# GpSimd takes over the subtraction for 36 weight pieces beside a 31-tap convolution

## The reference, cut to what matters

```
h   = rms_norm(x, norm_mix_pre)                  # 256 x 2048
u   = h @ w_in_2                                 # 2048 -> 4352 = 3*768 + 2*768 + 512
u_a, u_b, u_c = split(u)
val, gate = split(u_b); glu = val * sigmoid(gate)
y_b = silu(layer_norm(causal_conv31(glu) + bias))  # 31 taps per channel, 768 channels
y_a = b_gate * causal_conv3(c_gate * v)            # from u_a
y_c = pooled means of u_c, times pool_w
y   = concat(y_a, y_b, y_c) @ w_out_2
```

## Time and profile before

| | us |
|---|---|
| median of 3 runs | 2858.72 |
| profiled execution, its own time | 2861.59 |
| span of its instructions | 2859.5 |
| TensorE busy (matmul) | 2675.6 |
| VectorE busy | 1665.1 |
| ScalarE busy | 1158.2 |
| GpSimd busy | 10.6 |

### The profile page before, as it was taken

The page is one execution under the profiler, slowest core; times in us unless marked ns, Lnnn a source line. Parts: engine busy times, 40 slices in busy tenths (PEclk is TensorE's granted clock), DMA queues, the critical chain, the costliest instruction groups (busy, mean ns, idle before and its releaser), DMA issues.

```text
span 2859.5 us, 45648 instructions
## 1 busy us (share of the span) xinstructions
PE 2675.6 (94%) x20456; PEld 2552.4 (89%) x20456; DVE 1665.1 (58%) x1955; ACT 1158.2 (41%) x1266; POOL 10.6 (0%) x23
## 2 busy tenths in 40 slices
PE   6899999999989999999999799849699999999996
PEld 3488898899989999999999699839599999999996
DVE  4266666387767545455454457954566546654664
ACT  3222555343335434344343343323444434443442
POOL 0000000000000000000000000000000000000000
PEclk9899999999999999999999899969799999999998
DMA  9766565487765655555555244415155555555451
GB/s 375 306 234 229 199 220 192 162 297 273 293 235 215 225 180 184 186 179 190 177 185 184 103 148 154 153 51 188 55 181 181 188 181 188 177 186 183 177 192 45
DMA packets 76211, 546.91 MB, mean 191 GB/s; under 512 B 8720, under 2 KB 8848, under 8 KB 11120
## 3 DMA queue, kind: packets, MB, share of 16 engines
q1 hardware_dynamic: 73424, 533.53, 51.5%
q0 software_dynamic: 2304, 9.96, 0.9%
q10 hardware_dynamic: 288, 0.50, 0.1%
HBM read 538.72 MB, written 5.24 MB: 190 GB/s over the span
## 4 chain that ended last, share of the span: by engine, by line
PE 86%; DVE 8%; DMA 2%; ACT 2%; issue 1%; SPq 0%; POOL 0%; ACTq 0%; DVEq 0%
PE acc L264 24%; PE acc L266 24%; PE acc L268 24%; DVE cacc L1178 2%; PE mp L450 2%; DVE wlo L232 2%; DMA raw<-in_w_mod 2%; PE acc L284 2%; PE acc L285 1%; PE acc L286 1%; PE mp L286 1%; PE mp L284 1%; PE mp L285 1%; PE mp L333 1%; DVE macc L377 1%
## 5 line engine op out<-in xcount | busy, mean ns | idle before, releaser
L232 DVE TENSOR_TENSOR wlo<-raw,whi 128x1024 fp32r<-128x1024 f32 x813 | 984.2, 1223 | 875.3 <-ACT whi L222 873.1
L222 ACT ACTIVATE whi<-raw 128x1024 fp32r<-128x1024 f32 x813 | 853.6, 1058 | 1347.7 <-PE acc L268 1153.4
L264 PE MATMUL acc<-hh,whi 128*128 128x256 f32 x3616 | 1034.5, 286 | 37.0 <-issue 23.7
L266 PE MATMUL acc<-hl,whi 128*128 128x256 f32 x3616 | 1025.6, 284 | 0.0
L268 PE MATMUL acc<-hh,wlo 128*128 128x256 f32 x3616 | 1025.4, 284 | 0.0
L264 PEld LDWEIGHTS acc<-hh,whi 128*128 128x128 f32 x3616 | 695.9, 192 | 48.9 <-issue 39.2
L266 PEld LDWEIGHTS acc<-hl,whi 128*128 128x128 f32 x3616 | 696.2, 193 | 1.2 <-issue 1.0
L268 PEld LDWEIGHTS acc<-hh,wlo 128*128 128x128 f32 x3616 | 695.8, 192 | 0.0
L264 PE MATMUL acc<-mh,whi 128*128 128x256 f32 x2240 | 631.4, 282 | 16.5 <-DVE ml L1262 15.1
L268 PE MATMUL acc<-mh,wlo 128*128 128x256 f32 x2240 | 633.6, 283 | 0.0
L266 PE MATMUL acc<-ml,whi 128*128 128x256 f32 x2240 | 633.6, 283 | 0.0
(11 more groups left out here) (242 smaller groups left out, 1706.6 us busy)
## 6 DMA issues: line engine op xcount, KB each, us to landing
raw<-in_w_in SPq DMA_DIRECT2D x98, 1024.0 KB, 4.8
raw<-in_w_mod SPq DMA_DIRECT2D x96, 1024.0 KB, 5.0
raw<-in_w_up SPq DMA_DIRECT2D x88, 1024.0 KB, 4.8
raw<-in_w_mlp_in SPq DMA_DIRECT2D x64, 1024.0 KB, 4.8
raw<-in_w_mlp_out SPq DMA_DIRECT2D x64, 1024.0 KB, 4.7
raw<-in_w_down SPq DMA_DIRECT2D x44, 1024.0 KB, 4.7
raw<-in_w_out SPq DMA_DIRECT2D x32, 1024.0 KB, 4.8
raw<-in_w_fourier_out SPq DMA_DIRECT2D x8, 1024.0 KB, 4.9
```

What stands on the lines that cost most here:

```text
L222: nc.scalar.activation(whi[:, r, :], raw_slot(k)[:, 2 * GC * j:2 * GC * (j + 1)], ACT.Copy)\
L232: nc.vector.tensor_tensor(wlo[:, r, :], raw_slot(k)[:, 2 * GC * j:2 * GC * (j + 1)], whi[:, r, :].bitcast(f32), ALU.subtract).then_inc(S[" ...
L264: nc.tensor.matmul(dst, whi[:, r, cols], hi[:, kt, :], start=begin, stop=False, skip_group_check=True)
L266: nc.tensor.matmul(dst, whi[:, r, cols], lo[:, kt, :], start=False, stop=False, skip_group_check=True)
```

## The change

GpSimd gets a loop at the end of its program that makes the low halves of 36 pieces in a row, from piece `P_TAPS` on. Its instruction is the same subtraction of 128x1024 values. It waits for `hi_n` as VectorE did, and also for `lo_n` to have reached p, so that the count goes on from VectorE's last piece and then from its own. `P_TAPS` is four above the first piece of u_a, since the low halves run four pieces ahead: the 36 are the last 32 pieces of `w_in_2` and the first 4 of `w_out_2`.

VectorE no longer makes any piece in that stretch. In each of the four groups it goes through 48 steps of the convolution without a piece between them, then waits for the group and copies it. Before the last copy it waits until `lo_n` shows all 36 pieces.

```diff
+P_TAPS = len(PIECE) - 2 * (16 + 22 * 4 + 44) - 36 + 4
...
+        def pool_piece(pool, p):
+            k, j = PIECE[p]
+            pool.wait_ge(S["hi_n"], p + 1)
+            pool.wait_ge(S["lo_n"], p)
+            nc.gpsimd.tensor_tensor(wlo[:, p % 4, :], raw_slot(k)[:, 2 * GC * j:2 * GC * (j + 1)],
+                                    whi[:, p % 4, :].bitcast(f32), ALU.subtract).then_inc(S["lo_n"], 1)
...
+            for p in range(P_TAPS, P_TAPS + 36):
+                pool_piece(pool, p)
...
             for g in range(0, 2):
                 for b in range(2):
-                    C(behind=taps(g, 48 * b))
+                    assert st.p == P_TAPS + 8 * (2 * g + b)
+                    add = taps(g, 48 * b)
+                    for _ in range(8):
+                        add()
+                    st.p += 8
+                    st.e += 8
                     group_done(dve, st)
                     nc.vector.tensor_copy(uT[:, ds(8 * g + 4 * b, 4), :], tiles(acc[b][:, :]))\
                         .then_inc(acc_free[b], 1)
-            C(4)
+            st.p += 4
+            st.e += 4
+            dve.wait_ge(S["lo_n"], st.p)
             group_done(dve, st)
```

## The result

The changed kernel takes 2893.91 us (median of 4 runs, 2891.48 to 2896.98) against 2858.95 us for the kernel before (4 runs). The ratio is 1.0121, with a 95% interval of 1.0103 to 1.0138. The forecast was 2891.8 us. The profiled execution took 2895.22 us and has a span of 2893.4 us.

The account below looks back on a forecast made before the run. VectorE was taken to bound the 118.4 us convolution stretch. There 79.2 us of GpSimd pieces plus 72.3 us of convolution make 151.5 us, 33.1 us longer, so 2858.72 us becomes 2891.8 us; range 2844 to 2912 us.

Parts of the forecast that it names:

- What is removed: VectorE's queue in the convolution stretch: 36 pieces by 1.135 us, 40.9 us, leaving 77.5 us of convolution and copies.
- Taking turns: Convolution stretch: GpSimd pieces and VectorE's two-SBUF-input steps exclude each other by whole instructions; 33.1 us longer, chance 0.58.
- The size: Convolution stretch: 79.2 us of pieces plus 72.3 us of convolution, 151.5 us against 118.4 us now.
- the price of a piece: One low-half subtraction on GpSimd: 2.2 us, halfway between two streams and three, with ends 0.95 and 2.66 us.
- two inputs in turn: A GpSimd subtraction reading its inputs one after the other, with the output beside them, would cost 1.8 us.
- the overlap at hand-overs: Between a GpSimd piece and a convolution step: could hide 0.13 us at most 36 times, or cost as much; left out.
- The stalls: TensorE in the convolution stretch: about 47 us idle in three or four blocks over 10 us, waiting for a copy, clock dropping.
- VectorE first: Rival: GpSimd gets nothing while a group's 48 steps run; stretch 26.3 us longer, 2885.0 us, chance 0.08.
- free passage: Rival: in the convolution stretch the engines don't meet and TensorE sets the pace; gain 12.6 us, 2846.1 us, chance 0.20.
- Less the 11.0 us of waits this becomes 1853.9 us: End of TensorE's last piece in the stretch, about 1864.9 us, moved earlier by its waits for low halves.

Follow-up runs that it names:

- the sums in PSUM: Changed kernel with the convolution's two running sums in PSUM instead of SBUF, one extra copy per tile: 2843.16 us, ratio 0.9935 to the kernel before.
- the fill: Kernel before, VectorE still making all pieces, plus 36 unused GpSimd fills of 1024 values beside the convolution: 2863.66 us, ratio 1.0007.
- The copy: Kernel before, VectorE still making all pieces, plus 36 unused GpSimd copies of 1024 values, one SBUF input each: 2885.89 us, ratio 1.0088.
- the run with 16 pieces: Changed kernel with only 16 of the 36 pieces on GpSimd, in the first two groups, VectorE making the other 20: 2877.06 us, ratio 1.0054.
- no steps: Changed kernel without the convolution's 174 multiply-adds, which are replaced by signals: 2838.89 us, ratio 0.9925 to the kernel before.
- the run with the later wait: Changed kernel with running sums in PSUM and VectorE's wait for all 36 low halves moved behind the mixer: 2838.99 us, ratio 0.9918.

## Why the prediction was right, step by step

**What is removed.** 40.9 us of VectorE's queue were forecast, and 77.5 us to remain. The run with the sums in PSUM shows about the same: VectorE was busy for 80.63 us in the stretch, with 2.5 us of added copies in it. One slip is in how I divided the 77.5 us. The last copy, 0.61 us, starts at 1869.80 us, where the stretch ends, so the convolution had 72.9 us and not 72.3, and the sum should have been 152.1 us.

**Taking turns** is shown, by three independent runs: take the second SBUF input away from VectorE and the loss is gone (0.47 us a step); take the inputs away from GpSimd (the fill) and it is gone (0.458 us); keep both, without any dependence, and it is there (2.10 us for a step that waited). The rule of the Trainium skill that I named (SBUF — State Buffer, § Who interferes with whom) agrees with each of the three, also in that a GpSimd instruction that only writes leaves the steps alone.

**The size** came out right (74.0 us forecast to be added, 154.2 - 77.5 = 76.7 measured) with two errors that cancel. The first is the price of a piece. I took 2.2 us; it is 2.40 us, and 2.55 us from start to start. I had reasoned that no row shows GpSimd hiding one stream behind another. The copy shows it: one stream in and one out took 1.04 us, hardly more than the fill's 0.954. By that a subtraction would be the 1.8 us of two inputs in turn. It took 1.89 us with one tensor and 2.40 us with three, so my 2.2 us was near for no good reason. My estimate of 2.25 us from the figure of the Trainium skill (GPSIMD Engine Reference, § 3.1 Elementwise) was also too low for the three tensors of this change. The second is how a piece meets VectorE. I hid the copies beside pieces, 5.2 us, and left out the overlap at hand-overs as at most 4.7 us. In fact all copies fell where GpSimd was idle, and in each turn one step went along at no cost of its own: 36 x 2.55 + 77.5 - 36 x 0.39 = 155.3 us. Counted from VectorE's side, 36 instructions were held, one for each piece: 33 multiply-adds at 2.61 us (2.15 us more than a free one), two of L1182 at 2.38 and one of L1175 at 2.50 us. This is 2.13 us for each piece (76.7/36), which my 2.2 us met by luck.

**The stalls** were forecast as about 47 us of idle time in three or four blocks of over 10 us, with the clock falling. Measured: TensorE idle for 154.22 - 103.61 = 50.6 us, of which 37.0 us lay in three waits for a copy, the longest 15.8 us, and 12.9 us in a fourth before the small matmuls; TensorE's granted clock was 0.50, the lower level of 1.2 GHz, from 1800 to 1810 us. They cost nothing beside the sum, as the run with 16 pieces shows.

**VectorE first** did occur once. The piece that started at 1847.22 us lasted 7.95 us, through 15 undisturbed steps from 1847.25 on, while each other piece got in after at most one step. Why this one didn't is open. It made the loss no smaller: like the others it held one instruction of VectorE in the end, the addition L1175 at 1852.95 us, for 2.50 us.

**What was wrong: the rival "free passage"**, in its size. I gave it 2846.1 us, a gain of 12.6 us; where passage was free the gain was 18.2 and 22.4 us (the sums in PSUM, and no steps). The step that failed is "Less the 11.0 us of waits this becomes 1853.9 us". That row doesn't hold all that TensorE lost: for the same 808 matmuls its modelled busy time was 104.82 us before and 98.10 us in the run with the sums in PSUM, so some of the loss was counted as busy. The count gives it rightly. The stretch has 796 large matmuls (808 less the 12 small ones), at 0.12 us each, as the chain shows them where TensorE isn't held up:

```profile
1840.09 0.12 PE acc L273
1840.21 0.12 PE acc L275
```

That is 95.5 us. With the sums in PSUM TensorE took 95.4 us from the end of the gated product (1748.54) to the small matmuls (1843.89), where the kernel before had taken 113.4 us (1751.45 to 1864.87), 18.0 us more, 7.0 more than the row of waits.

## What to carry to other kernels

Before work is moved from VectorE to GpSimd, count on both sides the instructions with inputs in SBUF. Here nearly each GpSimd instruction that read SBUF held one of VectorE's instructions for nearly its whole length. A piece took 1.135 us from VectorE's queue and held it for 2.13 us, and that is the loss of 1 us a piece. Such a move pays only if it takes more from VectorE than it holds. With one operand of VectorE's chain in PSUM, the same move paid. To see what TensorE could do in a stretch, multiply its count of matmuls by their spacing where nothing holds it, and don't subtract a row of waits.

## What the runs showed of the hardware that was not expected

VectorE's multiplication by a column (L1182) has one SBUF input, and I had not counted it among what meets GpSimd. It waited too: 1067 ns on the mean, two of six at 2.38 us and the others at 0.40 to 0.41. It did so even beside fills, which only write. VectorE's groups in that run:

```profile
L1183 DVE TENSOR_SCALAR cacc<-uT,par 128x255 f32<-128x255 f32 x6 | 3.6, 603 | 0.0
L1179 DVE TENSOR_SCALAR cacc<-uT,par 128x256 f32<-128x256 f32 x6 | 3.2, 526 | 0.1
```

These were 349 and 410 ns in the kernel before, while the two-input steps kept 458 ns. With its output in PSUM the same multiplication (L1184 of the run with the sums in PSUM) took 0.54 to 0.55 us in all six cases, each beside a reading piece. It takes the same in the kernel before with the sums in PSUM, where GpSimd is idle, so none was held:

```profile
L1184 DVE TENSOR_SCALAR mp<-uT,par 128x256 f32<-128x256 f32 x6 | 3.3, 546 | 0.2
```

So what makes an instruction of VectorE meet one of GpSimd is not only its number of inputs; for this multiplication it also mattered where the output lies.

A step beside a reading instruction of GpSimd ends a little after it. It takes longer than a free one by the other's duration less about 0.25 us: 0.79 us beside copies of 1.04, 1.64 beside subtractions of 1.89, 2.15 beside those of 2.40 us. The first piece took 3.0 us in each run in which GpSimd makes pieces. In each of these runs it began 1.0 us into the gated product, which has two inputs in SBUF and takes 1.76 us, and it ended 2.3 us after the product's end (1751.14 and 1753.41 us in the changed kernel). So here it was the piece that waited, as the last one did in the run with the later wait.
